# Routing the experts head by head over all tokens, with half of the modulation moved into a feed-forward

## The reference, cut to what matters

```
q = (ht @ wq).reshape(T, 8, 2, 128)                     # 8 heads, two halves: 16 query units
sc = einsum('thpd,hpnd->thpn', q, subkeys)              # 128 scores per half
v1, i1 = top_k(sc[:, :, 0], 16); v2, i2 = top_k(sc[:, :, 1], 16)
cand = v1[..., :, None] + v2[..., None, :]              # 256 pairs per token and head
best, pos = top_k(cand, 16)
experts = (i1[pos // 16] * 128 + i2[pos % 16])          # of 16384 experts
gates = softmax(best)
out[t] = sum_k gates[t,k] * gelu(u[experts[t,k]] . h[t]) * v[experts[t,k]]
mod = silu(c) @ ada_w[l] + ada_b[l]                     # 6 sections of 1024 for each of 2 layers
```

## Time and profile before

| | |
|---|---|
| runs | 2853.68, 2858.34, 2859.15 us; median 2858.34 us |
| profiled execution, first to last instruction | 2856.6 us |
| busy: PE | 2803.3 us (98%) |
| busy: PEld, DVE | 2401.8 us (84%), 1773.6 us (62%) |
| busy: POOL, ACT | 1627.5 us (57%), 979.1 us (34%) |
| HBM | 174 GB/s over the span |

### The profile page before, as it was taken

How to read it: one execution, slowest core, us unless ns; L and a number is a source line. 1 busy time by engine, 2 the same in 40 slices (tenths; PEclk the granted TensorE clock), 3 DMA queues, 4 the chain that set the end, 5 groups by cost and what they waited for, 6 DMA issues and landing times.

```text
span 2856.6 us, 39244 instructions
## 1 busy us (share of the span) xinstructions
PE 2803.3 (98%) x14439; PEld 2401.8 (84%) x14439; DVE 1773.6 (62%) x2743; ACT 979.1 (34%) x1452; POOL 1627.5 (57%) x1653
## 2 busy tenths in 40 slices
PE   8899999999999999999999999999999999999999
PEld 6798888888888899999998796588888878988887
DVE  6578999996652377878887965854333353433333
ACT  4542333322223333333334546743222232331121
POOL 5444878787777478877751431025555536455553
PEclk9999999999999999999999999999999999999999
DMA  6942444488984689999993321013222222222231
GB/s 201 342 150 84 140 152 143 141 331 316 328 298 155 232 310 332 349 363 342 366 362 135 108 67 49 1 42 103 97 99 99 89 82 96 89 96 96 93 102 69
DMA packets 195767, 503.40 MB, mean 176 GB/s; under 512 B 31672, under 2 KB 83000, under 8 KB 195000
## 3 DMA queue, kind: packets, MB, share of 16 engines
q1 hardware_dynamic: 108624, 343.09, 34.8%
q10 hardware_dynamic: 52200, 91.23, 9.1%
q0 software_dynamic: 34816, 67.41, 6.7%
HBM read 432.76 MB, written 64.68 MB: 174 GB/s over the span
## 4 chain that ended last, share of the span: by engine, by line
PE 87%; POOL 4%; DVE 3%; DMA 2%; issue 2%; ACT 1%; SPq 0%; ACTq 0%; DVEq 0%
PE ps L662 27%; PE ps L663 27%; PE ps L664 27%; POOL picked L576 2%; PE ps L1019 2%; POOL value_rows L584 2%; PE ps L1039 1%; DMA unit_raw<-w_units 1%; PE ps L1030 1%; DMA value_rows<-w_units,row_at 1%; PE ps L950 1%; PE ps L860 1%; DMA abuf<-act_dram 0%; DVE std L1649 0%; DVE swa_small L1811 0%
## 5 line engine op out<-in xcount | busy, mean ns | idle before, releaser
L558 POOL TENSOR_TENSOR unit_lo<-unit_raw,unit_hi 128x256 fp32r<-128x256 f32 x984 | 761.1, 810 | 767.3 <-ACT unit_hi L1183 766.7
L662 PE MATMUL ps<-hn_hi,unit_hi 128*128 128x512 f32 (+1 forms) x2352 | 911.5, 388 | 17.8 <-DVE hn_lo L1750 10.5
L664 PE MATMUL ps<-hn_hi,unit_lo 128*128 128x512 f32 (+1 forms) x2352 | 897.2, 381 | 0.0
L663 PE MATMUL ps<-hn_lo,unit_hi 128*128 128x512 f32 (+1 forms) x2352 | 897.0, 381 | 0.0
L1183 ACT ACTIVATE unit_hi<-unit_raw 128x1024 fp32r<-128x1024 f32 x486 | 506.1, 1055 | 449.8 <-DMA unit_raw<-w_units 349.3
L590 POOL DMA_INDIRECT gate_dram<-gate_sums,gate_at x384 | 471.5, 1228 | 136.5 <-issue 126.9
L662 PEld LDWEIGHTS ps<-hn_hi,unit_hi 128*128 128x128 f32 x2352 | 443.2, 188 | 117.7 <-issue 18.3
L663 PEld LDWEIGHTS ps<-hn_lo,unit_hi 128*128 128x128 f32 x2352 | 443.5, 189 | 86.6 <-issue 4.5
L664 PEld LDWEIGHTS ps<-hn_hi,unit_lo 128*128 128x128 f32 x2352 | 443.1, 188 | 85.2
L1887 DVE TENSOR_TENSOR unit_lo<-unit_raw,unit_hi 128x1024 fp32r<-128x1024 f32 x240 | 292.3, 1222 | 107.5 <-ACT unit_hi L1183 104.9
L662 PE MATMUL ps<-gp_hi,unit_hi 128*128 128x384 f32 x1024 | 344.6, 337 | 12.7 <-DVE gp_lo L2049 12.6
(11 more groups left out here) (284 smaller groups left out, 3791.2 us busy)
## 6 DMA issues: line engine op xcount, KB each, us to landing
unit_raw<-w_units SPq DMA_DIRECT2D x486, 512.0 KB, 3.8
araw<-ada_units SPq DMA_DIRECT2D x96, 512.0 KB, 5.7
act_dram<-stage ACTq DMA_DIRECT2D x32, 1024.0 KB, 6.7
gate_dram<-zero SPq DMA_DIRECT2D x8, 3072.0 KB, 23.9
abuf<-act_dram ACTq DMA_DIRECT2D x32, 768.0 KB, 7.6
gbuf<-gate_dram ACTq DMA_DIRECT2D x15, 1536.0 KB, 21.3
gate_dram<-gate_sums,gate_at POOLq DMA_INDIRECT x384
x<-x_t SPq DMA_DIRECT2D x8, 256.0 KB, 6.1
```

The source lines that it names most:

```text
L558: last = nc.gpsimd.tensor_tensor(lo[:, u % RING, cols], raw[:, u % RING, cols], hi[:, u % RING, cols].bitcast(F32), ALU.subtract)
L662: mm(dst, wh, ah, start=start, stop=False)
L663: mm(dst, wh, al, start=False, stop=False)
L664: return mm(dst, wl, ah, start=False, stop=stop)
```

## The change

The routing goes head by head for all four tiles. `best_pairs(h)` forms the pairs of one head for four tiles and takes the 16 best, `place_pairs(h)` decodes them and makes the expert numbers, `join_gates(h)` norms the gates and adds up those of equal experts, and raises `heads_joined` for each of tiles 1 to 3. Head 0 goes beside the query units: its three steps follow DVE's query units 2, 4 and 6; ACT's exponentials for it follow query unit 6. The other seven heads follow the last query unit, with `join_gates` one head behind. DVE now releases the scores' PSUM bank (`tk_done`) in the middle of its work on a query unit and makes the key units' `lo` from u = 12 (was 20).

POOL makes the `lo` of units up to query unit 9. Then it waits for the first join of head 0, and gives the `lo` of the next twelve units (query units 10 to 15, key units 0 to 5) one at a time, each followed by four scatters. The key units 6 to 11 come after that without scatters, then the other 336 scatters, head by head, no longer paced by `hi_ready`.

Of the modulation, six sections stay beside the key units, now loaded from u = 70 and added up from u = 75. The six of the second layer move into FF0: SP loads their pieces between the units of FF0's groups, DVE adds them up in `weighed` (eight pieces per section, three sections per four groups), PE sums each in four matmuls. DVE's loop over FF0's groups is written out.

```diff
-ADA_LOW = 59
-ADA_LOAD = 54
-LOW_FROM = 20
+EARLY = 6
+ADA_LOW = 75
+ADA_LOAD = 70
+LOW_FROM = 12
+FIRST_LOWS = 10
+BEST_LOWS = (0, 1, 2, 2, 2, 2, 2, 2)
+PLACE_LOWS = (0, 1, 2, 2, 2, 2, 2, 2)
+JOIN_LOWS = ((0, 0, 0), (0, 1, 0), (1, 1, 1), (1, 1, 1), (1, 1, 1), (1, 2, 1), (1, 2, 1), (2, 2, 2))
+BEST_AT = [LOW_FROM + sum(BEST_LOWS[:h + 1]) + sum(PLACE_LOWS[:h]) + sum(sum(n) for n in JOIN_LOWS[:max(0, h - 1)])
+           for h in range(8)]
+FIRST_EXP = 6
@@ POOL
-            low_range(U_WIN + 14, U_PEER + LOW_FROM)
+            low_range(U_WIN + 14, U_WQ + FIRST_LOWS)
             pool.wait_ge(zeroed, 16 * ZEROS)
-            for n, (t, h) in enumerate(SCATTERS):
-                pool.wait_ge(heads_joined, PEER_HEADS * (t - 1) + h + 1)
+            def scatters(h, t, low=None):
+                pool.wait_ge(heads_joined, (TT - 1) * h + t)
                 if h:
                     pool.wait_ge(scattered[t - 1], 16 * TOPK * h)
                 for k in range(TOPK):
-                    burst, of = (TOPK * n + k) // BURST, TOPK * len(SCATTERS) // BURST
-                    if k % BURST == 0:
-                        pool.wait_ge(hi_ready, U_PEER + LOW_FROM + STEPS * burst // of + 2)
+                    if low is not None and k % BURST == 0:
+                        low_part(low + k // BURST)
                     scatter(t, TOPK * h + k)
+            for t in range(1, TT):
+                scatters(0, t, low=U_WQ + FIRST_LOWS + BURST * (t - 1))
+            low_range(U_WQ + FIRST_LOWS + BURST * (TT - 1), U_PEER + LOW_FROM)
+            for h in range(1, PEER_HEADS):
+                for t in range(1, TT):
+                    scatters(h, t)
@@ ACT
+                if n == FIRST_EXP:
+                    head_exp(0)
...
-                if u in EXP_AT:
+                for h in range(1, PEER_HEADS):
+                    if u == BEST_AT[h] - 1:
+                        head_exp(h)
@@ DVE
+            FIRST_HEAD = {2: best_pairs, 4: place_pairs, 6: join_gates}
+            for n in range(2 * PEER_HEADS):
+                top_keys(n)
+                if n in FIRST_HEAD:
+                    FIRST_HEAD[n](0)
...
-            for t in ORDER[:-1]:
-                select(t)
-                join_gates(t)
-            select(ORDER[-1])
+            best_pairs(1)
+            place_pairs(1)
+            for h in range(2, PEER_HEADS):
+                best_pairs(h)
+                join_gates(h - 1)
+                place_pairs(h)
+            join_gates(PEER_HEADS - 1)
@@ DVE, inside join_gates(h)
+                dve.wait_ge(gx_done, h + 1)
...
+                for t in range(1, TT):
...
+                    V.sem_inc(heads_joined, 1)
+                    lows(JOIN_LOWS[h][t - 1])
@@ PE, first feed-forward
+            def late_sum(g, i):
+                pe.wait_ge(ada_used, i * (3 * DC) + (EARLY * DC + DC * (g + 1)))
+                pe.wait_ge(x_done, i * (4 * DC) + (X_FF0 + DC * g + 5))
+                rows = late_acc[:, g].rearrange("p (b q r) -> p q b r", q=4, r=32)
+                for q in range(4):
+                    last = mm(ps[32 * q:32 * q + 32, 4, 0:2 * P].rearrange("p (b r) -> p b r", r=32),
+                              pick_c[:, 0, :], rows[:, q], start=True, stop=True)
+                last.then_inc(ada_summed, 1)
@@ DVE, weighed() of the first feed-forward, for each k of 2
+                        if group is not None and group % 4 and k:
+                            late_turn(3 * (group // 4) + group % 4 - 1)
+                        if group is not None and group % 4 < 3:
+                            late_parts(group, k)
```

More of the change, by code:

```diff
@@ L894, in key_unit @@
                 s, after = (u - ADA_LOW - 3) // 4, (u - ADA_LOW - 3) % 4
-                if after == 0 and 0 <= s < SECTIONS:
+                if after == 0 and 0 <= s < EARLY:
                     ada_sum(s, i)
@@ L1124, in gate_up @@
                             project(u + 2 * k + a, ps[:, 2 * a + k, :], hn_hi, hn_lo, per=24, i=i)
+                            if L == 0 and i is not None and g >= 2 and k + a == 0:
+                                late_sum(g - 2, i)
                 def down(g, u, i=None):
@@ L1128, in down @@
                     pe.wait_ge(ff_p, n if i is None else i * 8 + n)
+                    if L == 0 and i is not None and g >= 1:
+                        pe.wait_ge(ada_turned, i * 3 + (EARLY + g))
                     for m in range(DC):
@@ L1861, in _, with top_keys @@
             V.memset(pick_c[:, 1, 1:2], 1.0).then_inc(cact_ready, 1)
-            for n in range(2 * PEER_HEADS):
+            def top_keys(n):
                 dve.wait_ge(sc_ready, n + 1)
@@ L1926, in lows, with head_slots @@
                 key_lows[0] += n
-            def select(t):
-                between = SELECT_LOWS[t]
-                gate = sel[:, t, 2, :].rearrange("p (h k) -> p h k", k=TOPK)
-                pair = [vals[:, t].rearrange("p (h two) k -> p h two k", two=2)[:, :, v, :] for v in range(2)]
-                place = [idxF[:, t].rearrange("p (h two) k -> p h two k", two=2)[:, :, v, :] for v in range(2)]
-                link(V.tensor_tensor(cand[:, :, :].rearrange("p h (i j) -> p h i j", i=TOPK),
-                                     pair[0].unsqueeze(3).broadcast_to(full), pair[1].unsqueeze(2).broadcast_to(full),
-                                     ALU.add))
-                for h in range(PEER_HEADS):
-                    last = V.max(best[:, h, 0:8], cand[:, h])
+            def head_slots(h):
+                return slice(TOPK * h, TOPK * (h + 1))
@@ L1940, in select, with best_pairs @@
+            def best_pairs(h):
+                link(V.tensor_tensor(cand[:, :, :].rearrange("p t (i j) -> p t i j", i=TOPK),
+                                     vals[:, 2 * h].unsqueeze(3).broadcast_to([P, TT, TOPK, TOPK]),
+                                     vals[:, 2 * h + 1].unsqueeze(2).broadcast_to([P, TT, TOPK, TOPK]), ALU.add))
+                for t in range(TT):
+                    last = V.max(best[:, t, 0:8], cand[:, t])
                 link(last)
-                for h in range(PEER_HEADS):
-                    V.max_index(pos[:, TOPK * h:TOPK * h + 8], best[:, h, 0:8], cand[:, h])
-                    last = V.match_replace(cand2[:, h], best[:, h, 0:8], cand[:, h], LOWEST)
+                for t in range(TT):
+                    V.max_index(pos[:, t, 0:8], best[:, t, 0:8], cand[:, t])
+                    last = V.match_replace(cand2[:, t], best[:, t, 0:8], cand[:, t], LOWEST)
@@ L1944, in select @@
                 link(last)
-                lows(between[0])
-                for h in range(PEER_HEADS):
-                    last = V.max(best[:, h, 8:16], cand2[:, h])
+                lows(BEST_LOWS[h] // 2)
+                for t in range(TT):
+                    last = V.max(best[:, t, 8:16], cand2[:, t])
                 link(last)
-                for h in range(PEER_HEADS):
-                    last = V.max_index(pos[:, TOPK * h + 8:TOPK * h + 16], best[:, h, 8:16], cand2[:, h])
-                link(V.tensor_tensor(gate, best[:, :, :],
-                                     best[:, :, 0:1].broadcast_to([P, PEER_HEADS, TOPK]), ALU.subtract))
+                for t in range(TT):
+                    last = V.max_index(pos[:, t, 8:16], best[:, t, 8:16], cand2[:, t])
@@ L1959, in select @@
-                for v, where in enumerate((iF, jF)):
-                    link(V.tensor_tensor(dec[:, :, :], iota[:, 0:TOPK].unsqueeze(1).broadcast_to([P, SLOTS, TOPK]),
-                                         where[:, :].unsqueeze(2).broadcast_to([P, SLOTS, TOPK]), ALU.is_equal))
-                    d4 = dec[:, :, :].rearrange("p (h k) a -> p h k a", k=TOPK)
-                    link(V.tensor_tensor(d4, d4, place[v].unsqueeze(2).broadcast_to(full), ALU.mult))
-                    link(V.reduce_sum(sel[:, t, v, :], dec[:, :, :], AX_X))
-                    lows(between[2 + v])
```

245 lines of the change are left out of this document (153 added, 92 removed).

## The result

The changed kernel takes 2902.7 us (median of 4 runs, 2898.3 to 2905.0), the kernel before on the same chip 2856.9 (4 runs). The ratio is 1.0166, 95% interval 1.0139 to 1.0194. The profiled span is 2901.7 us at a granted clock of 0.992 (before 2856.6 at 0.996): 45.1 us more. The forecast was 2903. Its largest term holds to half a microsecond; two smaller terms were wrong in opposite directions, and part of the agreement is luck.

What follows compares the result with a forecast made beforehand. The prediction took PE, busy 98% of the span, as the bound. Its terms, 36 for POOL, 9 for DVE beside the key units and 0 for FF0, gave 2858.3 + 45 = 2903 us, range 2888 to 2920.

Steps and rivals of the forecast that it cites:

- POOL, 36: Query unit 10 to key unit 6: POOL's wait for head 0's join and its scatters between `lo` delay PE 36 us.
- The room in the blocks: POOL's blocks of `lo` and four scatters: 1.5 to 2.4 us of room per unit absorbs 1.7 us lost to half clock.
- the bound of 50: Upper end for the delay by key unit 6, with POOL's scatters at their mean of 1.58 us: 50 us.
- DVE beside the key units, 9: Key units 40 to 58: DVE's routing makes its `lo` late and PE waits; 10 us summed, 9 taken, ends 0 and 15.
- FF0, 0: First feed-forward: moved modulation sums balance for PE and DVE's added work fits; 0 taken, bounded by 0 and 8 us.
- POOL alone: Rival, 25%: only POOL's 36 us counts, DVE is cheaper head by head and never late beside the key units; 2894 us.
- FF0 holds PE up: Rival, 8%: in FF0 modulation pieces land late or DVE's longer chain meets PE; 45 + 8 = 53 us, 2911.
- scatters at their mean: Rival, 15%: POOL's blocks are heavier, scatters taking their mean time; 50 + 9 = 59 us, 2917.
- not slower: Rival, 7%: first join before 228.7 us and scatters costing POOL only issue leave PE at its pace; 2855 to 2858 us.
- The cap of 3.1 us: Seam from key to value units: PE's one wait of 3.12 us there is the most that can be won.
- 2.27 us of idle: A later PE idle after the seam, read as doing nothing visible to the next matmuls' times.

Runs made afterwards that it cites:

- e2_pool: The changed kernel with POOL making every `lo` up to key unit 11 first and all 384 scatters after that: 2864.3 us, ratio 1.0032.
- e3_wait: e2_pool with POOL again waiting for head 0's first join before query unit 10's `lo`, still no scatters between the `lo`: 2881.8 us, ratio 1.0095.
- e4_exp: e2_pool with ACT making head 1's exponential after key unit 8 instead of 12: 2862.1 us, ratio 1.0016.
- e8_first_hi: e4_exp with FF0's memsets before `weighed(0)`, activation and gate loads after key unit 124, first value unit's `gp_hi` before ACT's key unit 127: 2848.1 us, ratio 0.9974.

## Why the prediction was right, and where it was not

**POOL, 36: right.** 16.4 + 20.0 = 36.4. The join was due at 241.4 and came at 245.13, of which 2.2 is the offset that this execution had from the start. The other 1.5 is DVE's own work: it began `best_pairs(0)` 0.7 late and took 9.9 us for it (8.9 predicted) and 10.8 for each two query units (10.3); `place_pairs(0)` took 8.0 (8.7) and the join 1.3 (1.6). In this stretch it never waited for scores (L1921). PE was 16.4 late, not 12.7: 1.6 for the join and the `lo`, about 2 for the lower clock after 14.1 us of idle (0.50 granted from 248.05 to 251.50). The room in the blocks then took this back, as said. Blocks were 7.81 where I took 7.87; 46 of the 48 scatters took 0.95 to 0.99, the other two 1.23 and 1.47, so the bound of 50 at their mean of 1.58 didn't come near. e2_pool and e3_wait measure both parts by themselves.

**DVE beside the key units, 9: mechanism right, term mis-sized.** It was 4.3: 2.0 of waits, the rest clock (last section). The wait for head 1's exponential was 5.9 (6.3 predicted) and e4_exp shows that it is what makes DVE late. From the start of the `lo` of unit 12 to that of unit 56 DVE needed 261.5 us, not 268.3, and PE came to unit 12 20.2 us after that start (19.9 in the prediction: 18.7 and the `lo`'s 1.2). The size that failed is `place_pairs`, 8.7 each as half of a tile's: DVE's groups from 355 to 612 us give

```profile
L2014 DVE TENSOR_TENSOR dec<-con,ijF 128x2048 f32<-128x2048 f32 x7 | 16.0, 2292 | 0.2
L2021 DVE TENSOR_REDUCE sel<-dec 128x128 f32<-128x2048 f32 x7 | 16.0, 2286 | 0.2
L2019 DVE TENSOR_TENSOR dec<-dec,idxF 128x2048 f32<-128x2048 f32 x7 | 16.0, 2285 | 0.0
```

6.9 us for the three long operations and 0.8 for the small ones, 7.7 in all: seven times 1.0 too much. The rows that it came from the earlier trace rows were read while POOL worked on its `lo`: the four long two-input operations there took 2.48 to 2.73 us, and 2.29 in the later tiles of the kernel before. I said so and still took only 1 off the sum of 10.

**FF0, 0: wrong.** The sums were balanced rightly (-4.8, +4.8), though "24 of the 112 matmuls" is miscounted: the profile has two records for each of these matmuls, 112 before and 64 and 48 after. A group with a sum takes 33.4 us, 0.8 more than the 32.6 that I expected of all. What failed is the sentence that both of DVE's pieces of work fit in FF0: I followed the work that was moved there and not the memsets moved past `weighed(0)`, on which PE waits for `cact_ready`. That cost 5.3 us. Every instruction of a moved step counts, even two memsets of 0.17 us.

**The sum.** 36.4 + 4.3 + 5.3 is 46.0, and 2.2 at the start less 3.1 from key unit 127 to FF0, which no run ties to the change, makes 45.1. The terms that failed, 4.7 too much and 5.3 too little, cancel: that part of the agreement is luck. "POOL alone" (2894) missed DVE's term and the FF0 wait; "FF0 holds PE up" had the place and 5.3 of its 8 us, but not the cause, since neither late pieces nor their adding held PE; "scatters at their mean" fell by their 0.96; "not slower" fell by the join at 245. The cap of 3.1 us on what the seam can give left out the lower clock behind the wait: value unit 8 comes 4.9 us sooner after key unit 127 in e8_first_hi than in the kernel before.

## What to carry to other kernels

A wait put into an engine's queue costs what stands behind it: here routing finished earlier, the scatters began earlier, and all of it was bought with `lo` of the units that PE needed next. Put work that nobody waits for behind work that somebody does, and follow a semaphore's increment when the code around it moves, however short it is. The change as it stands costs 45 us; with POOL's order, one exponential and two memsets moved, and in two kernels the load as well, the same idea has medians 6 to 9 us (0.2 to 0.3%) below the kernel before. No single run can show that, since one stage differs by more from execution to execution, and the traces put the gain in that stage and not in the moved work.

## What the runs showed of the hardware that was not expected

**A wait of 1.8 us can cost as much again.** After the late `lo` of key unit 51 (start, us):

```profile
589.28 0.50 PE L693 MATMUL ps<-hn_hi,unit_hi 128*128 128x512 f32 x1 [1.82 <-DVE unit_lo L1938]
...
590.08 0.40 PE L693 MATMUL ps<-hn_hi,unit_hi 128*128 128x512 f32 x1
590.32 0.58 PE L694 MATMUL ps<-hn_lo,unit_hi 128*128 128x512 f32 x1
...
591.12 0.63 PE L693 MATMUL ps<-hn_hi,unit_hi 128*128 128x512 f32 x1
```

```profile
589.20:593.00 3.80, 3.72 (x11) 2.96 (x12) 3.77 (x5) 0.00 (x0) 3.19 (x3) 0.65 0.25 86
```

The matmuls are 0.23 us apart at first, 0.43 from 590.69 to 593.68, then 0.23 again. Unit 51 was 3.8 us late, of which 1.8 is the wait. The prediction took 2.27 us of idle as harmless from one row, and the granted clock there is 1.00 from 1119 to 1126 us; here 1.82 was not. Four waits of 2 us in POOL's blocks say the same: after 1.96 us (to 302.5) and 2.08 (to 326.3) the next 4.5 us have a granted clock of 0.63 and 0.64, after 2.00 (to 318.5) and 2.02 (to 341.8) one of 1.00. So no length of idle in these traces separates the two. In POOL's blocks the same loss was hidden, here and in FF0 it counts.

**A scatter begun under a long two-input operation of DVE ends 0.83 us after that operation.** POOL and DVE of the changed kernel after 394 us:

```profile
394.12 2.29 POOL L613 DMA_INDIRECT gate_dram<-gate_sums,gate_at  x1 [0.30 <-issue]
396.71 0.96 POOL L613 DMA_INDIRECT gate_dram<-gate_sums,gate_at  x1 [0.30 <-issue]
397.98 1.89 POOL L613 DMA_INDIRECT gate_dram<-gate_sums,gate_at  x1 [0.30 <-issue]
400.17 0.95 POOL L613 DMA_INDIRECT gate_dram<-gate_sums,gate_at  x1 [0.30 <-issue]
```

```profile
393.28 2.29 DVE L2014 TENSOR_TENSOR dec<-con,ijF 128x2048 f32<-128x2048 f32 x1
...
396.75 2.28 DVE L2019 TENSOR_TENSOR dec<-dec,idxF 128x2048 f32<-128x2048 f32 x1
399.07 2.29 DVE L2021 TENSOR_REDUCE sel<-dec 128x128 f32<-128x2048 f32 x1
```

L2014 ends at 393.28 + 2.29 = 395.57 and the first scatter at 394.12 + 2.29 = 396.41; L2019 ends at 399.03 and the third scatter at 399.87. Of these two lines there are twelve such pairs, and in all the scatter ends 0.83 to 0.84 us after the operation. Under the reduction, as long but with one input, the scatter takes 0.95. Six scatters begin inside each line's operations: 2.3 to 2.6 us under L2014, 1.9 under L2019, .96 under L2021. Of the 83 scatters begun under DVE's `lo` (L1938) 81 end 0.83 us after it or later, and the two that begin together with it take 0.96. Two inputs are not the whole condition: both scatters begun under a `tensor_scalar` with one tensor input (L1954, 0.75 us) also end 0.83 after it. It is as if POOL's writing of descriptors waits for the whole operation. "SBUF — State Buffer", section "Who interferes with whom", of the Trainium skill infers that a two-input `tensor_tensor` leaves it alone; these rows say otherwise. Beside head 0's scatters DVE ran few such operations, and only two of the 48 took longer than 0.99 us; the longer, 1.47, began under one (L1984).
